# Expert layer: up-units 16 to 19 multiplied whole in full precision instead of as rounded halves

## The reference, cut to what matters

```python
q = (h @ w_q).reshape(b, s, PEER_HEADS, 2, PEER_HALF)
sc = jnp.einsum('bshpc,hpkc->bshpk', q, sub_keys)
top_v, top_i = lax.top_k(sc, PEER_TOPK)
cand_v = top_v[..., 0, :, None] + top_v[..., 1, None, :]      # 16 x 16 candidates
best_v, best_pos = lax.top_k(cand_v, PEER_TOPK)
gate = jax.nn.softmax(best_v, axis=-1)
act = jax.nn.gelu(jnp.einsum('chkd,cd->chk', u_tab[idx], hx))
out = jnp.einsum('chk,chkd->cd', gate * act, v_tab[idx])
```

## Time and profile before

| | before |
|---|---|
| median of 3 runs | 2105.24 us (2104.57 to 2108.31) |
| the profiled execution, whole | 2104.3 us |
| its span, first to last instruction | 2102.5 us |
| PE busy | 1914.5 us, 91% |
| DVE busy | 1293.0 us, 61% |
| ACT busy | 907.3 us, 43% |
| mean granted clock of PE | 0.952 |

### The profile page before, as it was taken

One profiled execution on the slowest core, in us unless ns is written; L12 is line 12 of the kernel. 1 busy time (PEld: TensorE's weight loads), 2 busy tenths in 40 slices (PEclk: granted clock), 3 DMA queues, 4 the chain that ended last, 5 costly groups with the idle time before them and its releaser, 6 DMA issues. The chain is left out here.

```text
span 2102.5 us, 31529 instructions
## 1 busy us (share of the span) xinstructions
PE 1914.5 (91%) x13115; PEld 1766.8 (84%) x13115; DVE 1293.0 (61%) x2018; ACT 907.3 (43%) x1168; POOL 11.7 (1%) x15
## 2 busy tenths in 40 slices
PE   7978897999899999999999969868899989788997
PEld 7968787899899999888888868758898879578976
DVE  5545764789888888655555558676465433445643
ACT  5445442144344343444444456555344333335532
POOL 0000000000000000000000000000000000000000
PEclk9988999999999999999999979888899999899999
DMA  6432334444434444455555523210354446314543
GB/s 231 165 141 84 117 141 160 141 161 181 141 142 160 141 149 153 167 213 200 186 193 199 185 101 134 96 41 1 120 180 154 188 161 211 80 60 146 186 164 136
DMA packets 47048, 310.70 MB, mean 148 GB/s; under 512 B 5166, under 2 KB 8750, under 8 KB 10448
## 3 DMA queue, kind: packets, MB, share of 16 engines
q1 hardware_dynamic: 45776, 306.73, 40.6%
q0 software_dynamic: 576, 1.72, 0.4%
q10 hardware_dynamic: 576, 0.55, 0.1%
HBM read 306.84 MB, written 2.13 MB: 147 GB/s over the span
## 5 line engine op out<-in xcount | busy, mean ns | idle before, releaser
L296 DVE TENSOR_TENSOR s_ring_lo<-s_ring,s_w_hi 128x2048 fp32r<-128x2048 f32 x240 | 549.7, 2291 | 310.9 <-ACT s_w_hi L290 310.3
L290 ACT ACTIVATE s_w_hi<-s_ring 128x2048 fp32r<-128x2048 f32 x240 | 457.6, 1907 | 121.1 <-PE bank L333 45.1
L333 PE MATMUL bank<-s_hT_hi,s_w_hi 128*128 128x256 f32 x2320 | 341.5, 291 | 14.7 <-PEq L347 9.8
L333 PE MATMUL bank<-s_hT_hi,s_ring_lo 128*128 128x256 f32 x2320 | 331.0, 286 | 10.3 <-DVE s_ring_lo L296 10.2
L333 PEld LDWEIGHTS bank<-s_hT_hi,s_w_hi 128*128 128x128 f32 x2320 | 306.9, 197 | 22.4 <-issue 21.5
L333 PEld LDWEIGHTS bank<-s_hT_hi,s_ring_lo 128*128 128x128 f32 x2320 | 304.1, 195 | 11.7 <-DVE s_ring_lo L296 11.7
L1310 PE MATMUL bank<-s_w_hi,s_hT_lo 128*128 128x512 f32 x1024 | 242.6, 389 | 0.3 <-issue 0.3
L1310 PEld LDWEIGHTS bank<-s_w_hi,s_hT_lo 128*128 128x128 f32 x1024 | 192.2, 188 | 40.2 <-issue 0.4
L333 PE MATMUL bank<-s_hT_lo,s_w_hi 128*128 128x256 f32 x1296 | 189.6, 291 | 0.0
L333 PEld LDWEIGHTS bank<-s_hT_lo,s_w_hi 128*128 128x128 f32 x1296 | 175.3, 201 | 0.0
L333 PE MATMUL bank<-s_x_r,s_w_hi 128*128 128x256 f32 x1024 | 143.7, 283 | 0.0
(11 more groups left out here) (377 smaller groups left out, 2194.1 us busy)
## 6 DMA issues: line engine op xcount, KB each, us to landing
s_ring<-weights SPq DMA_DIRECT2D x282, 1024.0 KB, 4.8
s_arena<-bias_by_distance SPq DMA_DIRECT2D x8, 384.0 KB, 6.4
s_arena<-bias_by_distance POOLq DMA_DIRECT2D x4, 384.0 KB, 8.7
s_arena<-mem SPq DMA_DIRECT2D x1, 1024.0 KB, 5.8
s_x<-x SPq DMA_DIRECT2D x1, 1024.0 KB, 13.5
x_away<-s_x SPq DMA_DIRECT2D x1, 1024.0 KB, 4.8
s_arena<-sub_keys SPq DMA_DIRECT2D x1, 1024.0 KB, 6.9
s_arena<-x_away SPq DMA_DIRECT2D x1, 1024.0 KB, 8.3
```

The costliest lines, as they stand in the source:

```text
L290: act.activation(k.w_hi[:, u % 2, :], k.ring[:, u % RING, :], ACT.Copy).then_inc(k.hi_ready, 1)
L296: dve.tensor_tensor(k.ring_lo[:, u % RING, :], k.ring[:, u % RING, :], plain(k.w_hi[:, u % 2, :]), ALU.subtract).then_inc(k.lo_ready, 1)
L333: last = pe.matmul(out[:, nb * S:(nb + 1) * S], w[:, c, nb * P:(nb + 1) * P], h[:, c, :], start=(n == 0 and c == 0), stop=(n == 2 and c == 7))
```

## The change

Units 16 to 19 of the up half (`WHOLE`) are multiplied by `unit_T` with `k.hT`, in plain fp32. ACT leaves out their `split_hi` and DVE their `split_lo`; `low()` passes over them, so that its next unit after 15 is 20. `split_unit` keeps the count `whole_units` right for the units behind. Nothing else moves: the number and the places of the calls of `low()` in the routing stay as they are, and so does the place of each `split_hi` behind its `gelu`.

```diff
+WHOLE = range(16, 20)
...
+    def split_unit(j):
+        k.whole_units = before + sum(1 for n in WHOLE if n < j)
+        return F + j
...
-                unit_T_split(k, pe, F + j, *h_pair, ps[j % 2])
+                if j in WHOLE:
+                    unit_T(k, pe, F + j, k.hT, ps[j % 2])
+                else:
+                    unit_T_split(k, pe, split_unit(j), *h_pair, ps[j % 2])
...
                 gelu(j)
-                split_hi(k, act, F + j + 2)
+                if j + 2 not in WHOLE:
+                    split_hi(k, act, split_unit(j + 2))
...
                 if low_done[0] < EARLY_R + 2:
-                    split_lo(k, dve, F + low_done[0])
+                    split_lo(k, dve, split_unit(low_done[0]))
                     low_done[0] += 1
+                    while low_done[0] in WHOLE:
+                        low_done[0] += 1
```

More of the change, by code:

```diff
@@ L1228, in peer @@
     own = k.steps
+    before = k.whole_units
+    def split_unit(j):
+        k.whole_units = before + sum(1 for n in WHOLE if n < j)
+        return F + j
     up_at = up_turns()
@@ L1299, in down @@
             def down(d, i):
-                v = F + PAIRS + d
+                v = split_unit(PAIRS + d)
                 pe.wait_ge(weighted_ready, i * 4 + (d + 1))
@@ L1352, in _ @@
                 if h == PEER_H - 1:
-                    split_hi(k, act, F)
-            split_hi(k, act, F + 1)
+                    split_hi(k, act, split_unit(0))
+            split_hi(k, act, split_unit(1))
             def gelu(j):
@@ L1385, in _ @@
                         gelu(j - 1)
-                        split_hi(k, act, F + j + 1)
+                        split_hi(k, act, split_unit(j + 1))
                 if g >= 1:
@@ L1404, in body @@
                 round_up(d + 1, bass.ds(i * 8 + 2 * (d + 1), 2))
-                split_hi(k, act, v + 1, turn=i * 4, ring_turn=i)
+                split_hi(k, act, split_unit(PAIRS + d + 1), turn=i * 4, ring_turn=i)
             downs(act, body)
@@ L1540, in _ @@
                     combine(up_at[g] - 1, max(g - 1, 0))
-                    split_lo(k, dve, F + up_at[g] + 1)
+                    split_lo(k, dve, split_unit(up_at[g] + 1))
                 if g >= 1:
@@ L1556, in body @@
                 take(d + 1, bass.ds(i * 8 + 2 * (d + 1), 2))
-                split_lo(k, dve, F + PAIRS + d + 1, turn=i * 4)
+                split_lo(k, dve, split_unit(PAIRS + d + 1), turn=i * 4)
             downs(dve, body)
+            k.whole_units = before
             dve.wait_ge(k.unit_done, F + 128)
@@ L2863, in program @@
     peer(k)
+    k.whole_units += len(WHOLE)
     k.stream_to = FIRST["gdn_qkv"] + RING
```

## The result

| | before | after |
|---|---|---|
| median | 2104.9 us (6 runs, 2102.68 to 2108.31) | 2119.81 us (6 runs, 2118.91 to 2120.89) |
| ratio to before | | 1.0069, interval 1.0057 to 1.0082 |
| span of the profiled execution | 2102.5 us | 2118.5 us |
| PE busy | 1914.5 us | 1919.0 us |
| DVE busy | 1293.0 us | 1284.4 us |

A forecast was written before the change was run, and what follows sets the result against it. The prediction took PE's start of the transposes, with PE full behind it, as the bound: 12.4 us later plus 2.2 of low clock, 14.6 on 2104.3, gives 2118.9; 0.9 for the median gives 2119.8 us, range 2116.5 to 2124.

The forecast's parts named there:

- The moment that counts: PE's start of the six transposes of the choices, 551.93 us before; PE has no slack behind it to recover a delay.
- The rival that the spreads make the delay good: Routing ends late but the spreads catch up: no change, about 2104 to 2109 us; chance 0.03.
- The whole unit, 6.91 us: Each of up-units 16 to 19 takes PE 6.91 us in plain fp32, back to back, against 5.76 for an undisturbed split unit.
- The rival of four full streams: Each whole unit on PE takes 7.68 us, unit 18 ends 2.3 us later, 2122.1 us in all; chance 0.04.
- The fillers left out: Without subtractions in DVE's routing turns 2, 3 and 4, and nothing in their place, chosen_ready would come at 537.9 us.
- The wait: DVE waits 22.2 us in turn 2 for unit 20's rounding; PE idles 17.5 us, transposes start 12.4 us later.
- The step not in the trace: On DVE in routing turn 4, product to sum without a filler, taken as 2.33 us, between 2.2 and 2.4.
- The clock: After its idle time PE runs the transposes and unit 20 at the low clock, losing 2.2 us (bounds 1.3 to 3.9).
- The rival of a longer spell: PE's low clock behind the pause lasts longer, costing 3.9 us in place of 2.2: 2121.5 us; chance 0.06.
- The sum: Over the whole kernel, 12.4 us of later transposes plus 2.2 us of low clock make 14.6 us, giving 2119.8 us.
- The gain of the products alone: PE's four whole units end at 546.81 us, so by them alone the transposes could start 5.1 us earlier.
- The rival of the opposite sign: DVE passes turn 2 without a wait, chosen_ready comes at about 538, 5.1 us gained: 2100.1 us; chance 0.04.

The follow-up runs named there:

- e1: The changed kernel with the calls of low() in turns 2, 3 and 4 of the routing's last loop taken out; 2099.9 us, ratio 0.9984 to the kernel before.
- e2: The changed kernel with unit 20 subtracted in turn 3 instead of turn 2, and unit 21 in turn 4; ratio 1.0044 to the kernel before.
- e3: The changed kernel with unit 20 subtracted in turn 4 and unit 21 behind chosen_ready; ratio 1.000 to the kernel before.
- e4: The changed kernel with fillers in place, but ACT rounding units 20 and 21 two units sooner; ratio 1.0034 to the kernel before.
- e6: The changed kernel with only units 16 and 18 whole, no filler in turn 3, units 20 and 21 subtracted behind chosen_ready; ratio 0.9975 to the kernel before.

## Why the prediction was right, point by point

- **The moment that counts.** Right. The spreads and downs took 305.0 to 305.1 and 362.1 us in each profile, whatever happened ahead of them: a later start was a later end. The rival that the spreads make the delay good fell with that.
- **The whole unit, 6.91 us.** Right: 520.74 to 548.5, where PE's 17.42 us of idle time begin, is 27.8 us for four, 6.94 each by the modelled end; in e1, where the transposes follow at once, it is 27.63 us from start to start, 6.91 each. The rival of four full streams (4 x 7.68 = 30.7 us) fell. The Trainium skill (FP8 and Floating Point Precision, TensorE Precision Notes) gives four passes for true fp32, and no time for a pass; here a plain matmul of 256 columns cost 0.432 us, 3.6 times the rounded one, so four passes of 0.120 us were too dear by 11%. How many passes it makes, no run shows.
- **The fillers left out.** Right: with none in the way, e1's routing ended at 539.3 on its clock, 112.1 us behind unit 0; the forecast's 537.9 is 112.2.
- **The wait.** Right in place, releaser and length: 22.12 us against 22.2, 17.42 us of pause on PE against 17.5, transposes 12.4 us later in both (13.9 against the other two profiles of the kernel before). e2 and e3 moved the wait's place in the routing, e4 its end, and the transposes followed to 0.1 us.
- **The step not in the trace,** product to sum without a filler, taken as 2.33: the profile after has 559.99 to 562.32, 2.33.
- **The clock.** Right in kind, over-sized. From the transposes to the first spread it took 574.07 - 565.95 = 8.12 us, against 6.61 before (551.93 to 558.54): 1.5 us lost, not 2.2. The granted clock of 0.63 over 5.0 us is 3.7 us at 1.2 GHz, where the earlier trace rows had 4.9 of work; the row that I took was one case of several. e2 lost 1.7 and e4 1.2 behind pauses of 10.44 and 7.85 us. The rival of a longer spell (3.9 us) fell.
- **The sum.** The stretch grew by 14.0 us for a forecast of 14.6, and by 15.4 against the other two profiles of the kernel before. That the median came out at the very number has luck in it: the parts outside were 2.0 us longer in the profile after, and the median of before with more runs is 2104.9, not 2105.24.
- **The gain of the products alone,** 5.1 us: true against the profile before, but that profile was the dearer sort of the kernel before. Against the other two it is 3.6. The term that was mis-sized is the slow spell in unit 18: I took it as a fixed part of the 32.76 us.
- **The rival of the opposite sign** (all waits go, none comes) is e1, made by hand: 2099.9 us against 2100.1 worked out. There is luck in that number too, since the kernel before had 2103.67 beside it and the ratio says a gain of 3.4 us, not 5.1. It needed one edit that the diff did not have.

## What to carry to other kernels

A filler is free only while what it waits for comes early; on an engine that takes its list in order, a filler that waits is a wait of everything behind it. When work is dropped from a sequence that fillers draw from by count, the remaining fillers slide to later items, and each new pair of place and item has to be checked for when its input can exist: here a call that had needed unit 14 finished came to need unit 18. Where two engines are both near full, it can pay to replace only as many items as the slower one needs relief for. Here a whole unit costs PE 1.15 us more than a split one, and PE ran without idle time in both e6 and e1: two whole units shortened the stretch by 7.4 us and four by 5.1 (ratios 0.9975 and 0.9984, whose intervals overlap). One whole unit, or three, was not tried.

## What the runs showed of the hardware that was not expected

The same pause of 2.48 us ahead of the same 32 matmuls left PE at full clock in one execution (7.55 us) and not in another (9.16 us). In the kernel before, behind waits of 1.40 and 3.04 us, the low clock came in unit 17 in two profiles; in the third unit 17 ran at full clock, and it came in unit 18, behind a further wait of 3.03 us. The Trainium skill (TensorE: Matmul & The Clock Gate, Part 1) says that the number of slow matmuls differs from run to run of one kernel, and the three profiles of the kernel before agree with that. So one profile is not enough to price a short pause: the layer's stretch of one and the same kernel was 132.8 us in one and 131.3 in the two others.
